# Long convolution taps moved to ScalarE in groups of six products, and twelve projection chunks computed from split rows and weights

## The reference

```python
n = rmsnorm(h, g_mix)
z = n @ w_in
conv_a, new_a = causal_dwconv(gate_c * xa, prev_a, w_conv_a)     # width 3, 384 channels
y_a = gate_b * conv_a
zb = jax.nn.gelu(z[..., o3:o4])
v = layernorm(zb[..., D_B:], g_ln_b, b_ln_b)
y_b = zb[..., :D_B] * chunk_mix(v, w_s, b_s)
glu = zc[..., :D_C] * jax.nn.sigmoid(zc[..., D_C:])
conv_c, new_c = causal_dwconv(glu, prev_c, w_conv_c)             # width 31, 384 channels
y_c = jax.nn.silu(layernorm(conv_c + b_conv_c, g_ln_c, b_ln_c))
h = h + concat(rmsnorm(y_a), rmsnorm(y_b), rmsnorm(y_c)) @ w_o
```

## Time and profile before

| | us |
|---|---|
| median of 3 runs | 1084.42 (1082.21 to 1085.61) |
| the profiled execution | 1082.2 |
| its span, first to last instruction | 1080.6 |
| TensorE busy | 1063.3 (98%) |
| VectorE busy | 886.3 (82%) |
| ScalarE busy | 682.0 (63%) |
| layer 0's mixer | about 9 to 107 |
| layer 1's mixer | about 338 to 440 |

### The profile page before, as it was taken

The page is one execution under the profiler, slowest core; times in us unless marked ns, Lnnn a source line. Parts: engine busy times, 40 slices in busy tenths (PEclk is TensorE's granted clock), DMA queues, the critical chain, the costliest instruction groups (busy, mean ns, idle before and its releaser), DMA issues.

```text
span 1080.6 us, 16287 instructions
## 1 busy us (share of the span) xinstructions
PE 1063.3 (98%) x5883; PEld 921.4 (85%) x5883; DVE 886.3 (82%) x1300; ACT 682.0 (63%) x875; POOL 43.8 (4%) x58
## 2 busy tenths in 40 slices
PE   9999999999999999999999999999999999999996
PEld 8888999999999888788888888888888888878786
DVE  5898866566677888569989899898998999999775
ACT  2117544344454116458888888888888878888674
POOL 1000000000000000000010000100100001003000
PEclk9999999999999999999999999999999999999998
DMA  8442645545444433439999999999999999999921
GB/s 336 153 156 82 232 170 217 204 168 212 167 156 156 152 110 116 185 127 391 352 383 398 335 412 364 367 399 363 390 370 359 403 363 379 377 366 405 385 88 41
DMA packets 24197, 291.50 MB, mean 270 GB/s; under 512 B 3160, under 2 KB 3192, under 8 KB 7376
## 3 DMA queue, kind: packets, MB, share of 16 engines
q1 hardware_dynamic: 21040, 280.32, 67.7%
q0 software_dynamic: 3104, 10.46, 2.8%
HBM read 283.98 MB, written 6.79 MB: 269 GB/s over the span
## 4 chain that ended last, share of the span: by engine, by line
PE 92%; DVE 4%; ACT 2%; DMA 1%; issue 1%; POOL 0%; DVEq 0%; ACTq 0%; POOLq 0%
PE bank L672 16%; PE bank L676 16%; PE bank L675 15%; PE bank L721 13%; PE bank L745 8%; PE bank L748 8%; PE bank L749 8%; PE bank L761 2%; PE bank L616 1%; DMA ring<-wstream 1%; DVE cv L1498 1%; PE bank L600 1%; PE bank L581 1%; DVE wlo L1324 0%; PE bank L783 0%
## 5 line engine op out<-in xcount | busy, mean ns | idle before, releaser
L1324 DVE TENSOR_TENSOR wlo<-ring,whi 128x1024 fp32r<-128x1024 f32 x384 | 459.9, 1221 | 49.6 <-ACT whi L919 42.8
L919 ACT ACTIVATE whi<-ring 128x1024 fp32r<-128x1024 f32 x384 | 404.3, 1059 | 85.3 <-PE bank L672 72.3
L672 PE MATMUL bank<-whi,gh_hi 128*128 128x512 f32 x512 | 204.4, 399 | 0.1
L676 PE MATMUL bank<-whi,gh_lo 128*128 128x512 f32 x512 | 199.7, 390 | 0.0
L675 PE MATMUL bank<-wlo,gh_hi 128*128 128x512 f32 x512 | 199.5, 390 | 0.0
L745 PE MATMUL bank<-gh_hi,whi 128*128 128x264 f32 x480 | 138.0, 288 | 0.0
L748 PE MATMUL bank<-gh_lo,whi 128*128 128x264 f32 x480 | 136.0, 283 | 0.0
L749 PE MATMUL bank<-gh_hi,wlo 128*128 128x264 f32 x480 | 135.9, 283 | 0.0
L672 PEld LDWEIGHTS bank<-whi,gh_hi 128*128 128x128 f32 x512 | 96.2, 188 | 21.9 <-DVE wlo L1324 3.5
L676 PEld LDWEIGHTS bank<-whi,gh_lo 128*128 128x128 f32 x512 | 96.1, 188 | 20.9
L675 PEld LDWEIGHTS bank<-wlo,gh_hi 128*128 128x128 f32 x512 | 96.3, 188 | 18.4
(11 more groups left out here) (278 smaller groups left out, 1373.5 us busy)
## 6 DMA issues: line engine op xcount, KB each, us to landing
ring<-wstream SPq DMA_DIRECT2D x130, 2048.0 KB, 8.4
y_rows<-work POOLq DMA_DIRECT2D x7, 512.0 KB, 8.2
ring<-wstream SPq DMA_DIRECT2D x1, 1536.0 KB, 10.2
h<-x_in SPq DMA_DIRECT2D x2, 528.0 KB, 4.1
y_out<-work SPq DMA_DIRECT2D x2, 528.0 KB, 3.0
par<-par_in SPq DMA_DIRECT2D x2, 494.5 KB, 6.9
c_sample<-xc POOLq DMA_DIRECT2D x2, 372.0 KB, 3.6
stc<-state_in SPq DMA_DIRECT2D x2, 360.0 KB, 9.4
```

The lines of the kernel that those rows point to most:

```text
L672: mm = pe.matmul(out[:, :], xh, whi[:, pos, cols_], start=(k == 0), stop=False)
L676: mm = pe.matmul(out[:, :], xl, whi[:, pos, cols_], start=False, stop=(k == last))
L919: nc.scalar.activation(whi[:, q % SPLITS, :], quarter_at(q), ACT.Copy).then_inc(S["hi"], 1)
L1324: v.tensor_tensor(wlo[:, q % SPLITS, :], quarter_at(q), whi[:, q % SPLITS, :].bitcast(F32), ALU.subtract).then_inc(S["lo"], 1)
```

## The change

1. Projection chunks 7 to 12 of zab are computed with `project`, from split rows `gh_hi`, `gh_lo` and split weights. ScalarE makes the high parts of the eight row tiles, VectorE the low parts, at the start of a layer (in layer 1 four of them ahead of the root). Their six quarters join the list of split quarters.
2. Of 31 taps VectorE computes the first 13 (`ALONE`) as before. The other 18 are nine groups (`PAIRS`) of two taps. For each group ScalarE writes six products (two taps, three chunks of channels; `tap_products`) into one of two sets of buffers, which lie in `sq` and `pp`. VectorE (`tap_pairs`) adds the second tap's three products to the first's in one instruction ("pair"), and the result to `cv` in another ("sum"); in its order stand pair 0, pair 1, sum 0, pair 2, sum 1, and so on. The products of group m wait for sum m - 2.
3. The copies of the states go from VectorE to ScalarE. GELU's table is loaded by a one-element instruction behind the last sigmoid. The semaphore of the constants takes in that of the ones.

```diff
+SPLIT_FROM = 7
+PAIRS = 9
+ALONE = TAPS_C - 2 * PAIRS
+EARLY_SPLIT = [NEED[_b["zab"] + _c] - 1 for _b in BASE for _c in range(SPLIT_FROM, N_ZAB)]
...
 def in_fp32(q):
-    return any(0 <= q - a < n for a, n in zip(FP32_FROM, FP32_Q))
+    return q not in EARLY_SPLIT and any(0 <= q - a < n for a, n in zip(FP32_FROM, FP32_Q))
...
+        products = [[sq[:, 2 + 3 * i:5 + 3 * i, 0:SEQ] for i in range(2)], [pp[:, 3 * i:3 + 3 * i, 0:SEQ] for i in range(2)]]
...
+                def projected(first, end):
+                    for c in range(first, end):
+                        if c < SPLIT_FROM:
+                            project_fp32(B["zab"] + c, 1, gz)
+                        else:
+                            project(B["zab"] + c, 1, *ghs, rows_lo if c == SPLIT_FROM else None, waited=KD * 2 * l)
...
+                high_rows(0, ROWS_FIRST[l])
                 guess_of(bank[4], root[:, :], rstd[:, :], (S["ms"], 1), S["root"])
+                high_rows(ROWS_FIRST[l], KD)
...
+                nc.scalar.activation(warm[:, 0:1], eps[:, :], ACT.Gelu_apprx_tanh)
...
+                def tap_products(m):
+
+                    if m == 0:
+                        act.wait_ge(S["glu"], 2 * CC)
+                    if m >= 2:
+                        act.wait_ge(products_added, PAIRS * l + m - 1)
+                    for i in range(2):
+                        k = ALONE + 2 * m + i
+                        for c in range(CC):
+                            nc.scalar.activation(products[m % 2][i][:, c, :], cpad[:, c, k:k + SEQ], ACT.Copy,
+                                                 scale=wc[:, c, k:k + 1]).then_inc(products_made, 1)
...
+                for c in range(2 * CB):
+                    tap_products(c)
                     act.wait_ge(acc_evac, B["zab"] + c + 1)
                     nc.scalar.activation(zb[:, c, :], ycat[:, c, :], ACT.Gelu_apprx_tanh).then_inc(S["gelu"], 1)
...
+                tap_products(4)
                 high_upto(dense_quarters(B["zab"] + 2 * CB + 1))
                 act.wait_ge(S["centred"], 1)
                 nc.scalar.activation(sq[:, 0:CB, :], lnb[:, :, :], ACT.Square).then_inc(S["squared"], 1)
+                tap_products(5)
                 guess_of(bank[5], root[:, :], rstd2[:, :], (S["variance"], 1), S["root_v"])
+                tap_products(6)
...
+                def tap_pairs(n):
+
+                    for _ in range(n):
+                        kind, m = pair_steps.pop(0)
+                        a, b = products[m % 2]
+                        if kind == "pair":
+                            dve.wait_ge(products_made, 2 * CC * (PAIRS * l + m + 1))
+                            nc.vector.tensor_tensor(a, a, b, ALU.add).then_inc(paired, 1)
+                        else:
+                            dve.wait_ge(paired, PAIRS * l + m + 1)
...
+                            nc.vector.tensor_tensor(cv[:, :, 0:SEQ], cv[:, :, 0:SEQ], a, ALU.add).then_inc(products_added, 1)
...
                 for c in range(2 * CB):
                     evacuate(B["zab"] + c, ycat[:, c, :])
-                    some_taps(4)
-                    low_upto(dense_quarters(B["zab"] + c))
-                    some_taps(3)
+                    some_taps((4, CC * ALONE, 0, 0)[c])
+                    tap_pairs(2 if c else 1)
...
                 for c in range(CA):
                     evacuate(at + 2 * c, pp[:, 6, :])
-                    some_taps(3)
+                    tap_pairs(2)
                     low_upto(dense_quarters(at + 2 * c))
-                    some_taps(3)
...
-                    some_taps(5)
+                    tap_pairs(1 if c == CA - 1 else 2)
```

More of the change, by code:

```diff
@@ L86 @@
 EARLY_Q = (40, 45)
+ROWS_FIRST = (0, 4)
 GROUP_ORDER = (2, 0, 1)
@@ L724, in project_fp32, with project @@
                     mm.then_inc(acc_ready, 1)
-            def project(first_chunk, n_chunks, hi, lo, waits=None, S=dense, after=None):
+            def project(first_chunk, n_chunks, hi, lo, waits=None, S=dense, after=None, waited=0):
                 for i in range(n_chunks):
@@ L845, in _ @@
                     else:
-                        project(B["wo"] + k, 1, *mix, S["y_lo"] if k == WO_FP32 else None)
+                        project(B["wo"] + k, 1, *mix, rows_lo if k == WO_FP32 else None, waited=KD * (2 * l + 1))
                     if l and k:
@@ L1465, in _, with low_rows @@
                 dve.wait_ge(par_loaded[l], 16)
[L1467 to L1471, removed]
-                    nc.vector.tensor_copy(xa[:, :, :, 0:TAPS_A - 1], sta[:, :, :, :])
-                    link(nc.vector.tensor_copy(xc[:, :, :, 0:TAPS_C - 1], stc[:, :, :, :]))
+                def low_rows(first, end):
+                    for k in range(first, end):
+                        dve.wait_ge(rows_hi, KD * 2 * l + k + 1)
+                        nc.vector.tensor_tensor(gh_lo[:, k, :], gz[k], gh_hi[:, k, :].bitcast(F32),
+                                                ALU.subtract).then_inc(rows_lo, 1)
+                low_rows(0, ROWS_FIRST[l])
                 reciprocal_root((S["root"], 1), bank[4])
+                low_rows(ROWS_FIRST[l], KD)
                 wc = cols(l, "w_conv_c").rearrange("p (c k) -> p c k", k=TAPS_C)
                 last = [0] * CC
+                pair_steps = []
+                for m in range(PAIRS):
+                    pair_steps.append(("pair", m))
+                    if m:
+                        pair_steps.append(("sum", m - 1))
+                pair_steps.append(("sum", PAIRS - 1))
+                def tap_pairs(n):
[7 more added lines that the diff above has]
+                            dve.wait_ge(paired, PAIRS * l + m + 1)
+                            if m:
+                                dve.wait_ge(products_added, PAIRS * l + m)
+                            else:
+                                dve.wait_ge(dve_step, max(last))
+                            nc.vector.tensor_tensor(cv[:, :, 0:SEQ], cv[:, :, 0:SEQ], a, ALU.add).then_inc(products_added, 1)
                 taps_done = [0] * CC
@@ L1485, in some_taps @@
                     for _ in range(n):
-                        open_chunks = [c for c in range(chunks) if taps_done[c] < TAPS_C]
+                        open_chunks = [c for c in range(chunks) if taps_done[c] < ALONE]
                         if not open_chunks:
@@ L1584, in mix_a @@
                     low_upto(dense_quarters(at + 2 * CA + c))
-                some_taps(TAPS_C * CC)
+                assert not pair_steps and taps_done == [ALONE] * CC
                 sample_taps()
```

66 lines of the change are left out of this document (37 added, 29 removed).

## The result

| | before | changed |
|---|---|---|
| median, us | 1083.61 (4 runs) | 1097.49 (1095.38 to 1098.37, 4 runs) |
| the profiled execution | 1082.2 | 1097.66 |
| its span | 1080.6 | 1096.0 |

The ratio is 1.0121, 95% interval 1.0108 to 1.0134: slower, 13.9 us between the medians.

The account below looks back on a forecast made before the run. TensorE looked like the bound, VectorE barely keeping pace; with the change, ScalarE and VectorE alternate. Two layers' 6.8 us make 13.6, added to 1082.2 give 1095.8; with 2.2 to the median, stated as 1097, range 1089 to 1107.

Parts of the forecast that it names:

- Products (c): ScalarE's six tap products per group, nine groups replacing eighteen VectorE taps: about 2.5 us a group.
- the lower bound: ScalarE's six products priced as copies without scale: 2.0 us a group, shift 3.6 us a layer, total 1089.4.
- Adds (d): VectorE's pair add and sum into cv for each group: 0.95 us for one, 1.8 for the two.
- Rounds: In the mixer's taps, ScalarE's products and VectorE's adds take turns and never overlap: 4.4 us a round.
- Stalls: TensorE's waits in layer 0's mixer: 4 us for the square, two for low quarters, 2.5 us for the taps.
- Shift: Delay of a layer at the end of the taps, 82.3 against 75.5: 6.8 us, layer 1 nearly the same.
- Rival 3 (clock): TensorE runs at 1.2 GHz after the mixer's stalls: 1 to 5 us a layer more, 1099 to 1107; chance 0.1.
- Rival 1 (TensorE stays the bound): TensorE keeps its 7.7 us saving from the split chunks, so faster, 1074.5 us; chance 0.05.
- by 72.7: Time in layer 0 when taps must be signalled for TensorE's saving to show: 75.89 less five chunks' 0.64.
- 0.4 us of margin: Layer 0 before the change: VectorE's last tap add ends at 75.47, TensorE starts averaging them at 75.89.
- The last chunk's 0.64 us are worth nothing: The last split projection chunk lies beside the chain behind the taps, so TensorE's 0.64 us saving there gains nothing.
- Part (a): Layer start: high parts and state copies on ScalarE, low parts on VectorE; first evacuation 1.3 us later, cost 0.

Follow-up runs that it names:

- splits alone: Against the changed kernel: all 31 taps back on VectorE, chunks 7 to 12 still split; 1093.31 us, ratio 1.008.
- sums first: Against the changed kernel: VectorE does each sum directly behind its pair, all else the same; 1085.26 us, ratio 1.0008.
- root first: Against sums first: chunks 8 to 12 split, guess of mixer B's root ahead of products 5, root and scaled rows ahead of pair 5; 1085.08 us, ratio 1.0013.
- products alone: Against the changed kernel: no chunk or row split, products still on ScalarE, same order of pairs and sums; 1089.96 us, ratio 1.0058.
- square first: Against the changed kernel: ScalarE squares lnb ahead of products 4 and of two high quarters; 1096.62 us, ratio 1.0119.

## Why the prediction was right, point by point

- **Time.** 1097.0 forecast, 1097.49 measured; slower, as given 0.90. That the two are only 0.5 us apart is luck. The prediction's own sum gives 1095.8 for the profiled execution, measured as 1097.66 (1.0 us of that is the later start of the first chunk), and with its 2.2 us to the median 1098.0, which it wrote down as 1097. The shift, too, is made up of two errors that nearly cancel (below).
- **Products (c).** 2.5 us for six: 2.50 in the trace. The same form in the earlier trace rows gave the price; neither bound was needed. (At the lower bound seven rounds lose 3.5 us and not 3.2, which moves that end from 1089.4 to 1088.8.)
- **Adds (d).** 0.95 and 1.8 for the two: the sum starts 0.88 behind the pair (46.61, 47.49), and the next product 0.99 behind that (48.48): 1.87.
- **Rounds.** Forecast pairs 4.4 apart by the order alone: 46.61, 51.01, 55.41. Undone by the order (1097.5 to 1085.3, and 1092.2 to 1077.9), so it is shown and not only argued. From pair 5 on the rounds aren't pure, as the walk had it: pairs 5 to 8 start 4.9, 5.2, 4.5 and 4.4 us after the one before, and quarters, root and scaled rows fill part of the waits.
- **Stalls.** Square: 4 us forecast, 3.63 measured; taps: 2.5 forecast, 2.06 measured; the low quarters forecast at 68.1, 72.5 and 76.9, ended about 68.4, 72.9 and 77.3 (starts 67.25, 71.72, 76.14, and some 1.15 each), but of two waits for them a layer only one, of 0.8 us, showed.
- **Shift.** 6.8 a layer forecast from taps to taps. Measured from the layer's first chunk: taps 72.01 for 65.85, 6.2; to the centring 6.7. The two parts are the rounds, 0.6 less than walked, and 0.5 that the forecast's sum didn't have: the half clock. That they nearly add up to 6.8 is chance.
- **Rival 3 (clock)** came in part: most of a chunk and one average at 1.2 GHz, 0.5 us a layer on the chain, where 1 to 5 were said. The size stayed small because the next wait absorbs most of it. The Trainium skill, "TensorE: Matmul & The Clock Gate", section "What's actually happening", has an idle array fall to half rate. By that rule the trace agrees: the stall of 3.63 us is followed by twelve matmuls in 4.52 us for 2.83.
- **Rival 1 (TensorE stays the bound)** would have needed the taps early; "by 72.7" was itself too lenient. As the kernel with chunks 8 to 11 split showed, they must come 1.1 us ahead of TensorE. For the same reason the reading "0.4 us of margin" was off: before, the centring stands at 78.05, where 75.89 + 1.61 = 77.50 was possible, so VectorE already came 0.55 late there. The sum wasn't hurt, since it went from taps to taps. Nor is it right that VectorE waits 0.36 us per chunk before: that is so in the first chunks of zab, from chunk 4 on it is mostly 0.5 to 0.8 (0.70, 0.68, 0.67, 0.48, 0.76).
- **"The last chunk's 0.64 us are worth nothing"** is in line with the kernels that leave chunk 12 in fp32, though none undid that chunk alone.
- **Part (a), cost 0**: with low rows and three quarters the taps came at most 0.3 us later than with none (63.30 and 63.01 us behind the first chunk).

What the experiments' expectations had wrong is one thing three times (splits alone, sums first, root first): VectorE's room was taken from the sum of its waits.

## What to carry to other kernels

Two sets of buffers decoupled the two engines here only when the instruction that frees a set wasn't queued behind one that waits for the other set: write both in-order queues side by side and follow one round before trusting busy sums. Work taken off the engine at the bound pays only as far as its partner at the next meeting is early, and that meeting is where the join is really consumed (here the centring, not the average). Such a trade between three engines is worth trying in several sizes: of those tried here, three of the six chunks, with adds in the right order, gave 0.5% gain, where the whole change lost 1.2%.

## What the runs showed of the hardware that wasn't expected

- TensorE's clock doesn't follow from the length of the last wait alone. Behind 3.63 us it ran at 1.2 GHz (4.52 us for 2.83). Behind waits of 1.73 (products alone, at the square) and 1.93 us (sums first, at the taps) it didn't. Behind 2.06 us at the taps the average over `cv` took 2.92 us in the changed kernel and only 1.60 in the one with the square first, with a wait of the same length. The traces differ in what came before: the changed kernel had waited 0.84 us for a low quarter up to 77.50, and the other had been at work from 66 to 80.9. Whether that made the difference wasn't tried.
- A wait moved is a slow stretch moved: with the square first TensorE waits 3.37 us up to 65.65 instead, and then the granted clock is 0.50 until 71.
- The first chunk began between 9.32 and 10.50 us in kernels with nearly the same code up to there; two traces should be compared from a common event behind it, not from the span's start.
